# A hybrid decoder layer on eight cores: the retention's transposes through DMAs of two blocks, with four gate groups held in PSUM

## What is computed

```python
def retention(q, k, v):   # after the rotary embedding; (B, S, H, 128), v (B, S, H, 256)
    scores = einsum('bnthd,bnshd->bnhts', q, k) * decay          # per chunk of 128 tokens
    inner  = einsum('bnhts,bnshe->bnthe', scores, v)
    kv     = einsum('bnshd,bnshe->bnhde', k * w_state, v)
    state  = state * chunk_decay + kv                            # over the chunks
    cross  = einsum('bnthd,bnhde->bnthe', q, r_prev) * cross_decay
    return standardize(inner + cross)                            # per head
yb = (ret * silu(r_z)) @ w_ob                                    # r_z: the gate
```

## Time and profile before

| what | us |
|---|---|
| median of 3 runs (lowest, highest) | 2753.83 (2751.45, 3262.64) |
| the profiled execution | 2780.39 |
| its span, on core 6 | 2778.8 |
| TensorE busy in the span | 2723.3 (98%) |
| DVE, ACT, POOL busy | 1108.8, 643.9, 204.8 |

### The profile page before, as it was taken

How to read it: one execution, slowest core, us unless ns; L and a number is a source line. 1 busy time by engine, 2 the same in 40 slices (tenths; PEclk the granted TensorE clock), 3 DMA queues, 4 the chain that set the end, 5 groups by cost and what they waited for, 6 DMA issues and landing times.

```text
span 2778.8 us, 42118 instructions; the slowest of 8 cores (2689.2 to 2778.8 us)
## 1 busy us (share of the span) xinstructions
PE 2723.3 (98%) x15098; PEld 1425.6 (51%) x15098; DVE 1108.8 (40%) x2685; ACT 643.9 (23%) x1543; POOL 204.8 (7%) x387
## 2 busy tenths in 40 slices
PE   5999999999999999999999999999999999999998
PEld 2646666655555666666544444444555544444443
DVE  1243442146665432222276343320566642221257
ACT  0121111035555111111100121110455531111100
POOL 3000000000000000000001000000000000000000
PEclk8879999999999999999999999999999999999999
DMA  9643434333224444343468754444244354544543
GB/s 143 125 99 66 64 62 84 66 57 60 52 52 98 69 76 69 69 69 69 97 189 182 143 80 76 76 84 76 46 73 78 75 99 85 83 73 74 86 119 133
DMA packets 66787, 241.53 MB, mean 87 GB/s; under 512 B 7696, under 2 KB 12944, under 8 KB 62992
## 3 DMA queue, kind: packets, MB, share of 16 engines
q0 software_dynamic: 56928, 193.49, 41.3%
q1 hardware_dynamic: 9648, 45.27, 4.5%
HBM read 413.31 MB, written 18.87 MB: 156 GB/s over the span
## 4 chain that ended last, share of the span: by engine, by line
PE 95%; DMA 2%; ACT 1%; issue 1%; DVE 1%; POOL 1%; DVEq 0%; ACTq 0%; POOLq 0%
PE ps_all L236 94%; PE ps_all L245 1%; DMA xT<-xT 1%; DMA ring<-w 1%; POOL ring L292 0%; ACT L257 0%; DVE xy_85 L264 0%; ACT aT L257 0%; POOL xT L292 0%; DVEq L971 0%; DVE zth_123 L264 0%; ACT zth_123 L257 0%; ACT zth_124 L257 0%; ACT zth_122 L257 0%; ACT zth_121 L257 0%
## 5 line engine op out<-in xcount | busy, mean ns | idle before, releaser
L236 PE MATMUL ps_all<-xT,ring 128*128 128x384 bf16 (+1 forms) x6400 | 1211.2, 348 | 0.6 <-ACT rs_65 L257 0.6
L236 PEld LDWEIGHTS ps_all<-xT,ring 128*128 128x128 bf16 x6400 | 624.0, 98 | 539.2 <-issue 2.5
L236 PE MATMUL ps_all<-ring,xT 128*128 128x512 bf16 (+1 forms) x3696 | 756.7, 365 | 30.1 <-DMA xT<-xT 28.0
L236 PEld LDWEIGHTS ps_all<-ring,xT 128*128 128x128 bf16 x3696 | 342.8, 101 | 386.3 <-issue 94.2
L236 PE MATMUL ps_all<-aT,ring 128*128 128x384 bf16 (+1 forms) x2560 | 484.0, 347 | 0.0
L292 POOL DMA_DIRECT2D ring<-w x368 | 196.3, 542 | 2443.4 <-PE ps_all L236 2011.7
L236 PEld LDWEIGHTS ps_all<-aT,ring 128*128 128x128 bf16 x2560 | 250.4, 98 | 219.8
L236 PE MATMUL ps_all<-ring,yT 128*128 128x512 bf16 x1088 | 235.2, 379 | 0.0
L236 PEld LDWEIGHTS ps_all<-ring,yT 128*128 128x128 bf16 x1088 | 106.5, 98 | 128.3
L275 DVE CAST yT<-ps_all 128x384 bf16<-128x384 f32 (+1 forms) x40 | 24.5, 612 | 205.8 <-PE ps_all L236 205.8
L264 DVE SCALAR_TENSOR_TENSOR ogb_130<-ogb_130,ps_all 128x384 f32<-128x384 f32 (+1 forms) x40 | 24.3, 607 | 183.7 <-PE ps_all L236 183.7
(11 more groups left out here) (253 smaller groups left out, 1887.3 us busy)
## 6 DMA issues: line engine op xcount, KB each, us to landing
ring<-w POOLq DMA_DIRECT2D x348, 512.0 KB, 6.4
xy_86<-x SPq DMA_DIRECT2D x9, 1024.0 KB, 6.1
out<-xy_86 SPq DMA_DIRECT2D x18, 512.0 KB, 2.6
xy_85<-x SPq DMA_DIRECT2D x8, 1024.0 KB, 5.3
out<-xy_85 SPq DMA_DIRECT2D x16, 512.0 KB, 2.8
xT<-xT POOLq DMA_DIRECT2D x8, 512.0 KB, 28.1
xT<-xT POOLq DMA_DIRECT2D x4, 1024.0 KB, 20.6
bias_71<-bias_s SPq DMA_DIRECT2D x2, 1024.0 KB, 11.9
```

What stands on the lines that cost most here:

```text
L236: return self.S.op("pe", lambda e: e.matmul(out, lhsT=l, rhs=r, start=start, stop=stop), [l, r], [out])
```

## The change

The four transposes of a step leave TensorE. `dma_tr` issues a transposing DMA on SP's queue: one moves q and k of a step ([128, 256], two blocks of 128x128) from `qkt` to `qkT`, right behind `rotary`; one moves both halves of the output from `ybp` to `aT`, right behind the normalization. The ACT copies out of banks 3 and 7 go too. `qkT` has six buffers in place of four, `p_mm` uses four banks in place of three, and the state update gets bank 7. The drain takes four gate groups in place of seven; these are held in banks 0 to 3 until all small work is recorded, and then their Tanh and products follow (`gate`). The scratch area grows by 2 KB per partition.

```diff
+    def dma_tr(self, key, out, in_):
+        self.S.op("sp", lambda e: e.dma_start_transpose(out=out, in_=in_), [in_], [out], key=key)
...
-            b = i % 3
+            b = i % 4
...
             self.tt(o[:, :, 64:128], ta[:, :, 1, :], tb[:, :, 0, :], ALU.add)
+            self.dma_tr("tq%d" % (i % 6), m.qkT[i % 6][:], o[:].rearrange("p j f -> p (j f)"))
...
         def small_pe(i):
-            a, b_, c_, y = i - 2, i - 3, i - 4, i - 7
-            if 0 <= a < N:
-                for j in range(2):
-                    self.tr(self.bank16(3)[:, j * 128:(j + 1) * 128], m.qkt[a % 6][:, j, :])
+            a, b_, c_ = i - 2, i - 3, i - 4
             if 0 <= c_ < N:
                 h, c = divmod(c_, n)
                 if not (last and c == n - 1):
-                    self.mm(self.bank(4)[:, 128:384], m.qkt[c_ % 6][:, 1, :], m.v[c_ % 6][:], True, True)
+                    self.mm(self.bank(7)[:, 0:256], m.qkt[c_ % 6][:, 1, :], m.v[c_ % 6][:], True, True)
             if 0 <= b_ < N:
-                self.mm(self.bank(4)[:, 0:128], m.qkT[b_ % 4][:, 1, :], m.qkT[b_ % 4][:, 0, :], True, True)
+                self.mm(self.bank(4)[:, 0:128], m.qkT[b_ % 6][:, 1, :], m.qkT[b_ % 6][:, 0, :], True, True)
             if 0 <= c_ < N:
                 ob = self.bank(5 + c_ % 2)[:, 0:256]
                 self.mm(ob, m.ST[c_ % 3][:], m.v[c_ % 6][:], True, False)
-                self.mm(ob, m.qkT[c_ % 4][:, 0, :], m.Rg[c_ % 3][:], False, True)
-            if 0 <= y < N:
-                for j in range(2):
-                    self.tr(self.bank16(7)[:, j * 128:(j + 1) * 128], m.ybp[y % 4][:, j * 128:(j + 1) * 128])
+                self.mm(ob, m.qkT[c_ % 6][:, 0, :], m.Rg[c_ % 3][:], False, True)
...
-            if 0 <= a < N:
-                self.act(m.qkT[a % 4][:].rearrange("p j t -> p (j t)"), self.bank16(3)[:, 0:256], AF.Copy)
...
             if 0 <= z < N:
+                h, c = divmod(z, n)
                 self.act(m.ybp[z % 4][:], self.bank(5 + z % 2)[:, 0:256], AF.Identity, scale=r[:, 0:1], bias=r[:, 1:2])
-            if 0 <= y < N:
-                h, c = divmod(y, n)
-                self.act(self.aT[:, 2 * h:2 * h + 2, c * 128:(c + 1) * 128],
-                         self.bank16(7)[:, 0:256].rearrange("p (j t) -> p j t", j=2), AF.Copy)
+                self.dma_tr("ty%d" % (z % 4), self.aT[:, 2 * h:2 * h + 2, c * 128:(c + 1) * 128], m.ybp[z % 4][:])
...
+        def gate(ct, c0, k, b):
+            tk = slice(c0 * CH, (c0 + k) * CH)
+            ps = self.bank(b)[:, 0:k * CH]
+            th = m.zth[self.rot("zt", 4)][:, 0:k * CH]
+            self.act(th, ps, AF.Tanh, scale=0.5)
+            self.stt(th, th, 1.0, ps, ALU.add, ALU.mult)
+            a = self.aT[:, ct, tk]
+            self.stt(a, a, 0.5, th, ALU.mult, ALU.mult)
+
         i = N
-        step = 0
+        held = []
+        self.nbank = 4
         for ct in range(16):
             s = self.w_take(1)
             for (c0, k) in self.sp:
...
+                b = i - N if i < N + 4 else self.next_bank()
+                self.group(self.bank(b)[:, 0:k * CH], [(m.ring[:, s, kt, :], self.xm(kt, c0, k)) for kt in range(KT)])
+                if i < N + 4:
+                    held.append((ct, c0, k, b))
                     small_pe(i)
                     small_post(i)
                     i += 1
...
+                    if i == N + 4:
+                        small_post(i)
+                        for g in held:
+                            gate(*g)
+                else:
+                    gate(ct, c0, k, b)
```

More of the change, by code:

```diff
@@ L658, in small_pe @@
                 self.mm(ob, m.ST[c_ % 3][:], m.v[c_ % 6][:], True, False)
-                self.mm(ob, m.qkT[c_ % 4][:, 0, :], m.Rg[c_ % 3][:], False, True)
-            if 0 <= y < N:
-                for j in range(2):
-                    self.tr(self.bank16(7)[:, j * 128:(j + 1) * 128], m.ybp[y % 4][:, j * 128:(j + 1) * 128])
+                self.mm(ob, m.qkT[c_ % 6][:, 0, :], m.Rg[c_ % 3][:], False, True)
         def small_post(i):
-            a, b_, c_, y = i - 2, i - 3, i - 4, i - 7
-            z = i - 5
+            a, b_, c_, z = i - 2, i - 3, i - 4, i - 5
             if 0 <= z < N:
@@ L676, in small_post @@
                 if not (last and c == n - 1):
-                    self.stt(m.U[:, h, :], m.U[:, h, :], float(self.gC[h]), self.bank(4)[:, 128:384], ALU.mult, ALU.add)
+                    self.stt(m.U[:, h, :], m.U[:, h, :], float(self.gC[h]), self.bank(7)[:, 0:256], ALU.mult, ALU.add)
             if 0 <= b_ < N:
@@ L699, in ret_stage @@
             if c == 1 and init:
-                state_init(h, (i - 1) % 3)
+                state_init(h, (i - 1) % 4)
             if i == 3:
@@ L856, in plan_memory @@
     s0 = top[0]
-    top[0] += 32768
+    top[0] += 34816
     assert top[0] <= nc.sbuf_usable_end, (top[0], nc.sbuf_usable_end)
@@ L868, in sub @@
             pos[0] += (size + 31) // 32 * 32
-            assert pos[0] <= s0 + 32768
+            assert pos[0] <= s0 + 34816
             return at(name, shape, dt, off)
@@ L894, in plan_memory @@
     m.v = [a("v%d" % i, [128, 256], BF16) for i in range(6)]
-    m.qkT = [a("qkT%d" % i, [128, 2, 128], BF16) for i in range(4)]
+    m.qkT = [a("qkT%d" % i, [128, 2, 128], BF16) for i in range(6)]
     m.ST = [a("ST%d" % i, [128, 128], BF16) for i in range(3)]
@@ L899, in plan_memory @@
     m.cs = a("cs", [128, NMAX, 128], F32)
-    assert a.pos[0] <= s0 + 24576
-    a = area(24576)
+    assert a.pos[0] <= s0 + 26624
+    a = area(26624)
     m.zth = [a("zth%d" % i, [128, 512], F32) for i in range(4)]
-    a = area(24576)
+    a = area(26624)
     m.yh = [a("yh%d" % i, [128, KT, 128], BF16) for i in range(2)]
```

## The result

| | median us | against before (95% interval) |
|---|---|---|
| before | 2754.67 | |
| changed | 2819.05 (2814.49 to 2821.93) | 1.0236 (1.0213 to 1.0259) |

The forecast was 2714 us, 40 us less; it became 64 us more.

What follows compares the result with a forecast made beforehand. The prediction took TensorE on the even cores as the bound; 29.9 us of removed transposes and 10.0 us of drain, 39.9 us together, came off the 2753.83 us median to give 2713.9 us, range 2700 to 2900 us.

Steps and rivals of the forecast that it cites:

- The step of 3.84 us: Retention: without two transpose pairs of 0.11 us each, a step falls from 4.06 to 3.84 us, 29.9 us over 136 steps.
- DVE does not become the bound: Retention steps: DVE works 3.05 us per step, below 3.84 us, so its waits shrink and TensorE still sets the time.
- the drain's 10 us: Drain after the retention: four held gate groups remove TensorE's waits and slower matmuls, 5.97 + 1.46 + 2.57 = 10.0 us.
- the sum itself: Whole kernel: 29.9 us from the transposes and 10.0 us from the drain, 39.9 us less.
- the latency: Retention, q and k transposes on SP's queue: 7.0 us allowed from issue to landing, 2.6 us taken from a store, hidden.
- that of DVE: Rival, retention: DVE and ACT set the step, only the drain's gain remains, 2744 us; 0.15 together with lateness beside weights.
- My throughput step: Retention, DMA engines: two transposes at 1.09 us each plus weights at 1.24 us take 3.4 of 3.84 us, so it fits.
- Late only beside the weights: Rival, retention: transposes in weight bursts make TensorE wait 4 us per head, 64 us, 2778 us; 0.15 together with DVE.
- The rival that I feared most: SP's queue, all 136 steps: it can't take two transposes per step, which becomes 5.2 us, 2899 us in total; chance 0.30.
- share of about 0.9: Sign of being right, retention steps: the DMA engines are busy for about 0.9 of the time, 3.4 of 3.84 us.
- the bound from below: Retention, a transpose's throughput: at the rate of a 512 KB store landing in 2.6 us, 64 KB take 0.33 us.

Runs made afterwards that it cites:

- e10_unheld: e7_lag_spread with the drain's gate groups not held, each group's Tanh and products following its small work at once; ratio to before 0.9888.
- e7_lag_spread: The changed kernel with weight units issued one at a time and scores, output and normalization one step later; 2711.58 us, ratio to before 0.985.
- e4_plain_copy: The changed kernel with plain DMA copies of the same 64 KB in place of the transposes; 2813 us, one run.
- e2_small_loads: The changed kernel with weight units loaded during the retention read to a sixteenth only; ratio to before 0.988, runs of 2710 and 2732 us.
- e1_spread: The changed kernel with a head's four freed weight units issued one at a time, behind steps 0, 2, 4 and 6; ratio to before 0.992.
- e8_pairs: The changed kernel with weight units issued two at a time, behind steps 0 and 4; 2731 us, one run.

## Why the prediction was wrong

**What was right.** The step of 3.84 us and TensorE full in it; that DVE does not become the bound; the drain's 10 us (e10_unheld); the sum itself: e7_lag_spread has every term of it, and its ratio of 0.985 is 41 us.

**The step that failed is the latency.** "A store of 512 KB on the same queue lands after 2.6 us: hidden." I took the quiet landing of the earlier trace rows for all steps, although had 11.0 us for the same store beside weight loads, and the earlier trace rows showed that such loads come with every head. Beside them a transpose took up to 14.4 us in the changed kernel. The reason by which I gave this case, together with that of DVE, only 0.15, that 64 KB are an eighth of the store's bytes, is false: the quiet landing depends little on the bytes (2.3 us for 64 KB, 2.6 us for 512 KB), and the late one neither (11.0 us for the store, up to 14.4 us for a transpose). What counts there is packets and turns. My throughput step did count packets, 1.09 us of the engines per transpose, but spread the weights over all steps, 1.24 us in each. They come in bursts in which they fill the engines (96.6% in the rows of the result), and SP's queue then gets one packet for each of theirs: some 6 us per transpose, with two in every 3.84 us.

**The rival had the place, and not the size.** "Late only beside the weights" gave one wait per head of 4 us, 64 us. Measured are 70.4 us. What it lacked is the clock: after such a wait the next matmuls run slower, 24.4 us in the `p_mm` groups alone and some 8 us beside them. With both the rival would have come to 2778 + 6 + 32 = 2816 us. The earlier trace rows had shown it (4.22 us against 2.76 after idle stretches), and I used it for the drain and not for the waits that I priced myself.

**The rival that I feared most is refuted for the quiet steps.** There the queue can take two transposes per step; in the bursts it can't, and that is what makes the waits. In the quiet stretch from 608 to 620 us, with no weight loads, the share of the engines is:

```profile
608.00:620.00 12.00, 12.00 (x65) 5.98 (x64) 8.56 (x35) 5.47 (x18) 0.00 (x0) 1.00 0.17 34
```

0.17 x 12 us for some six transposes is 0.33 us each; I had estimated 1.09 us from the earlier trace rows, three times too much, and 0.33 us is what the rate of the store gave as the bound from below. So the share of about 0.9 that I named as a sign never came: over the two stretches of steps it is 0.43 and 0.49. SP's issue went the other way (duration in ns, min/median/max):

```profile
L295 SPq DMA_TRANSPOSE aT<-ybp_118 x34: 1167/1170/1323, 585.3 to 2268.1; - x34
```

1.17 us in place of the 0.34 us of a plain issue; two of them are 2.3 of 3.84 us and delay nothing that shows. The Trainium skill's figure in "VectorE: DVE Perf Modes", section "The three transpose paths", 1309 ns for a 128x128 block by DMA, would have made 2.6 us per DMA one after the other, as an estimate; the trace, with 0.33 us of the engines, does not bear that out as a rate. The Trainium skill, "Advanced Engine Details and Errata", section "X-Bar Transpose (TRN2)", which has a transpose as fast as a regular DMA, is nearer: a plain copy landed after 1.9 us in the middle of e4_plain_copy's landings, a transpose after 2.3 us in e2_small_loads.

**What stays open.** The turns between the queues are read from counts of packets; no run changed the transposes' packets alone. e2_small_loads made the weights' packets a sixteenth at the same number of them (56928 in the program), and the lateness went, as turns would have it, but so would fewer bytes; against a share by bytes stands e1_spread. The Trainium skill, "DMA: Bandwidth & Descriptors", section "Issuing engines are not separate DMA queues", says that DMAs of SP and POOL run on the same 16 engines and interleave; the packets agree, 48 of each queue in one us of a burst. What makes a burst last longer, as in e8_pairs, is not shown.

## What to carry to other kernels

A DMA that takes the place of an instruction on the critical engine must be priced by its landing in the worst stretch in which it is issued, not by its median: look for what the other queue does there, count packets as well as bytes, and give the consumer that much slack or break up the burst. Spreading the other queue's loads and taking the result a step later cost nothing here and turned 64 us of loss into 41 us of gain. A long wait of TensorE that you price (here 3.25 us and more) can also cost clock behind it; add it.

## What the runs showed of the hardware

Transposing SBUF to SBUF by DMA, [128, 256] bf16, took 2.3 us from issue to landing in a quiet stretch, 1.17 us of SP for the issue, 288 packets and about 0.33 us of the 16 engines. Beside a burst of POOL's loads it took up to 14.4 us, a plain copy of the same bytes up to 13.8 us. Inside such a burst both queues moved the same number of packets, 48 each in one us, though SP's were of some 250 bytes (0.07 MB in 288) and POOL's of 4 KB (0.20 MB in 48). After waits of 3.25 to 4.74 us TensorE's next sixteen matmuls of 512 columns took 4.77 to 6.32 us in place of 3.62; with other matmuls in the place of most of the wait they took 3.62.
